# Broadcasting a norm's root with a diagonal and a ones matmul, and copying the rotary key with two DMAs, in a one-core transformer kernel

## The reference, cut to what matters

```python
def rms_norm(x, g):
    xf = x.astype(jnp.float32)
    y = xf * lax.rsqrt(jnp.mean(xf * xf, axis=-1, keepdims=True) + NORM_EPS)
    return (y * g.astype(jnp.float32)).astype(x.dtype)

    o = rms_norm(o, subln_g) * (1.0 - lambda_init)          # diff_attention, for each head
```

```python
    k_pe = apply_rope(proj[..., MLA_Q_RANK + MLA_KV_RANK:], cos, sin)
    ...
        sc = (jnp.einsum('bqhd,bkhd->bhqk', qn, k_nope)
              + jnp.einsum('bqhr,bkr->bhqk', qp, k_pe)).astype(jnp.float32) * scale
```

## Time and profile before

| | us |
|---|---|
| median of 3 runs (1761.54 to 1761.56) | 1761.56 |
| the profiled execution, its own time | 1761.54 |
| its span, first to last instruction | 1759.8 |
| TensorE busy | 1744.0 (99%) |
| VectorE busy | 1104.8 (63%) |
| ScalarE busy | 792.3 (45%) |

### The profile page before, as it was taken

How to read it: one execution, slowest core, us unless ns; L and a number is a source line. 1 busy time by engine, 2 the same in 40 slices (tenths; PEclk the granted TensorE clock), 3 DMA queues, 4 the chain that set the end, 5 groups by cost and what they waited for, 6 DMA issues and landing times.

```text
span 1759.8 us, 22818 instructions
## 1 busy us (share of the span) xinstructions
PE 1744.0 (99%) x8844; PEld 1471.2 (84%) x8844; DVE 1104.8 (63%) x1830; ACT 792.3 (45%) x1418; POOL 129.7 (7%) x129
## 2 busy tenths in 40 slices
PE   9999999999999999999999999999999999999998
PEld 7888888888888888888888888898888888888886
DVE  4689644343346766686755755756989777376375
ACT  6563522222235565545433433457766544144244
POOL 2003200000005100002000000022000200000000
PEclk9999999999999999999999999999999999999999
DMA  5212333333333221223333333323011233333341
GB/s 167 73 49 81 96 96 98 97 99 102 96 96 96 72 61 61 66 67 88 103 96 96 96 96 96 96 77 89 26 61 37 72 96 96 96 96 96 97 128 62
DMA packets 128355, 152.78 MB, mean 87 GB/s; under 512 B 9286, under 2 KB 101992, under 8 KB 128248
## 3 DMA queue, kind: packets, MB, share of 16 engines
q1 hardware_dynamic: 128088, 151.26, 28.1%
q10 hardware_dynamic: 160, 0.07, 0.0%
HBM read 148.61 MB, written 2.10 MB: 86 GB/s over the span
## 4 chain that ended last, share of the span: by engine, by line
PE 96%; DVE 1%; ACT 1%; issue 1%; POOL 0%; DMA 0%; ACTq 0%; POOLq 0%; DVEq 0%
PE bk L1801 23%; PE bk L1803 23%; PE bk L1802 23%; PE bk L1830 6%; PE bk L1832 6%; PE bk L1831 6%; PE bk L1806 4%; PE bk L1901 2%; PE bk L1868 1%; PE bk L1889 1%; PE bk L1891 1%; PE bk L1890 1%; ACT WH L2161 0%; PE bk L1934 0%; PE bk L1935 0%
## 5 line engine op out<-in xcount | busy, mean ns | idle before, releaser
L1801 PE MATMUL bk<-R,WH 128*128 128x512 f32 x1764 | 691.1, 392 | 1.2 <-DVE R L1972 0.9
L1803 PE MATMUL bk<-R,WL 128*128 128x512 f32 x1764 | 686.8, 389 | 0.0
L1802 PE MATMUL bk<-R,WH 128*128 128x512 f32 x1764 | 686.6, 389 | 0.0
L1966 DVE TENSOR_TENSOR WL<-RAW,WH 128x1024 fp32r<-128x1024 f32 (+4 forms) x278 | 343.7, 1237 | 483.9 <-ACT WH L2161 483.0
L2161 ACT ACTIVATE WH<-RAW 128x1024 fp32r<-128x1024 f32 (+4 forms) x278 | 288.0, 1036 | 595.6 <-PE bk L1803 540.0
L1801 PEld LDWEIGHTS bk<-R,WH 128*128 128x128 f32 x1764 | 331.2, 188 | 69.7 <-issue 2.5
L1803 PEld LDWEIGHTS bk<-R,WL 128*128 128x128 f32 x1764 | 331.1, 188 | 69.6
L1802 PEld LDWEIGHTS bk<-R,WH 128*128 128x128 f32 x1764 | 331.3, 188 | 67.0
L1830 PE MATMUL bk<-WH,R 128*128 128x512 f32 (+4 forms) x528 | 186.3, 353 | 0.2 <-ACT TOK L2218 0.2
L1832 PE MATMUL bk<-WL,R 128*128 128x512 f32 (+4 forms) x528 | 178.3, 338 | 0.0
L1831 PE MATMUL bk<-WH,R 128*128 128x512 f32 (+4 forms) x528 | 178.1, 337 | 0.0
(11 more groups left out here) (162 smaller groups left out, 1538.5 us busy)
## 6 DMA issues: line engine op xcount, KB each, us to landing
RAW<-in_ffn_w_up_dram SPq DMA_DIRECT2D x176, 256.0 KB, 3.1
RAW<-in_ffn_w_down_dram SPq DMA_DIRECT2D x44, 512.0 KB, 3.7
RAW<-in_w_gate_dram SPq DMA_DIRECT2D x44, 256.0 KB, 2.9
RAW<-in_w_up_dram SPq DMA_DIRECT2D x44, 256.0 KB, 3.1
RAW<-in_w_down_dram SPq DMA_DIRECT2D x22, 512.0 KB, 3.7
RAW<-in_da_w_qkv_dram SPq DMA_DIRECT2D x32, 256.0 KB, 2.9
RAW<-in_w_out_dram SPq DMA_DIRECT2D x8, 512.0 KB, 3.7
RAW<-in_da_w_qkv_dram SPq DMA_DIRECT2D x8, 512.0 KB, 3.7
```

The costliest lines, as they stand in the source:

```text
L1801: e.matmul(dst, lh, rh, start=start, stop=False)
L1802: e.matmul(dst, lh, rl, start=False, stop=False)
L1803: return e.matmul(dst, ll, rh, start=False, stop=stop)
L1966: e.tensor_tensor(low, RAW[:, r, 0:m], high.bitcast(F32), ALU.subtract).then_inc(on["wlo_dve"], 1)
```

## The change

Two steps are changed. First, `over` no longer transposes. A new VectorE step `diag` multiplies the identity (`IDN`) by each of the four columns of the root, which gives four diagonal 128 by 128 blocks in a slot of `FS`, and `over` multiplies a matrix of ones by each block in plain fp32 on TensorE. Second, `kpe` writes the rotary key's halves only into the first pair of key tiles (36 by 512 instead of 36 by 2048), and two DMAs copy them to the other three pairs of the first group and the four of the second. The `kups` lists are made in `mla_group` instead of ahead of it.

```diff
-    "over": {"pe": 1}, "over_copy": {"act": 1},
+    "diag": {"dve": 1}, "over": {"pe": 1}, "over_copy": {"act": 1},
...
-        return {"add": 682.0, "tap1": 743.0, "tap0": 743.0, "settle": 745.0, "root_in": 165.0, "root_ez": 165.0,
+        return {"add": 682.0, "tap1": 743.0, "tap0": 743.0, "settle": 745.0, "diag": 880.0, "root_in": 165.0, "root_ez": 165.0,
...
-        s_kpe = sem("s_kpe")
+        s_kpe = [sem(f"s_kpe{i}") for i in range(2)]
...
+                dg = yield from fslot()
+                st = yield step("diag", dst=FS[:, dg.i, 0:S], r=r.r1, after=counts([dg.free, r.rooted]))
                 bk = yield from bank()
-                st = yield step("over", bank=bk.i, r=r.r1, after=counts([bk.free, r.rooted]))
+                st = yield step("over", bank=bk.i, src=FS[:, dg.i, 0:S], after=counts([bk.free, st.dve]))
+                fsl.put(dg, st.pe)
...
+            dg = yield from fslot()
+            st = yield step("diag", dst=FS[:, dg.i, 0:S], r=r, after=counts([dg.free, rooted]))
             b3 = yield from bank()
-            st = yield step("over", bank=b3.i, r=r, after=counts([b3.free, rooted]))
+            st = yield step("over", bank=b3.i, src=FS[:, dg.i, 0:S], after=counts([b3.free, st.dve]))
+            fsl.put(dg, st.pe)
...
-            four = BK[b.i][64:100, :].unsqueeze(1).to_broadcast([36, 4, S])
-            lo = yield from halves(KT[64:100, 0:8:2, :], KT[64:100, 1:8:2, :], four, [st.pe], None, counts(kfree[0:8]))
-            for i in range(0, 8, 2):
-                lat.k[i] = lo
+            lo = yield from halves(KT[64:100, 0, :], KT[64:100, 1, :], BK[b.i][64:100, :], [st.pe], None, kfree[0] + kfree[1])
+            lat.k[0] = lo
             put_bank(b, lo)
-            while len(Ms[0].kups) < 4:
-                yield None
-            emit("kpe_copy", i0=8, i1=16, after=counts([lo, Ms[0].kups[3], kfree[8:16]]))
-            ready_at[id(s_kpe), 16] = at_time(Ms[0].kups[3]) + 8500.0
-            for i in range(8, 16, 2):
-                lat.k[i] = (s_kpe, 16)
+            for n, (i0, i1) in enumerate(((2, 8), (8, 16))):
+                emit("kpe_copy", n=n, i0=i0, i1=i1, after=counts([lo, kfree[i0:i1]]))
+                ready_at[id(s_kpe[n]), 16] = at_time(lo) + 4500.0 + 2000.0 * n
+                for i in range(i0, i1, 2):
+                    lat.k[i] = (s_kpe[n], 16)
...
-                        mm = turn(BK[st.bank][:, t * P:t * P + P], st.r[:, t:t + 1].to_broadcast([P, P]))
+                        mm = e.matmul(BK[st.bank][:, t * P:t * P + P], ONES, st.src[:, t * P:t * P + P], start=True, stop=True)
...
+                elif k == "diag":
+                    for done in st.after:
+                        w.wait_ge(*done)
+                    for t in range(4):
+                        i = e.tensor_scalar(st.dst[:, t * P:t * P + P], IDN, st.r[:, t:t + 1], None, ALU.mult)
+                    i.then_inc(on["diag_dve"], 1)
```

More of the change, by code:

```diff
@@ L1497, in kpe @@
             lat.ups.append(st.pe)
-            four = BK[b.i][64:100, :].unsqueeze(1).to_broadcast([36, 4, S])
-            lo = yield from halves(KT[64:100, 0:8:2, :], KT[64:100, 1:8:2, :], four, [st.pe], None, counts(kfree[0:8]))
-            for i in range(0, 8, 2):
-                lat.k[i] = lo
+            lo = yield from halves(KT[64:100, 0, :], KT[64:100, 1, :], BK[b.i][64:100, :], [st.pe], None, kfree[0] + kfree[1])
+            lat.k[0] = lo
             put_bank(b, lo)
-            while len(Ms[0].kups) < 4:
-                yield None
-            emit("kpe_copy", i0=8, i1=16, after=counts([lo, Ms[0].kups[3], kfree[8:16]]))
-            ready_at[id(s_kpe), 16] = at_time(Ms[0].kups[3]) + 8500.0
-            for i in range(8, 16, 2):
-                lat.k[i] = (s_kpe, 16)
-        for G in Ms:
-            G.kups = []
+            for n, (i0, i1) in enumerate(((2, 8), (8, 16))):
[3 more added lines that the diff above has]
+                    lat.k[i] = (s_kpe[n], 16)
         def mla_group(G, g, prior, before):
@@ L1515, in mla_group @@
             G.heads, G.turned = 0, True
-            G.tq, G.tk, G.qups, G.rope = [], [], [], None
+            G.tq, G.tk, G.qups, G.kups, G.rope = [], [], [], [], None
             in_line(G.V, G.O, *[[q] for q in G.Q])
@@ L1776, in sync_program @@
                     src = KT[64:100, 0:2, :].bitcast(F32).unsqueeze(1).to_broadcast(list(dst.shape))
-                    e.dma_start(dst, src).then_inc(s_kpe, 16)
+                    e.dma_start(dst, src).then_inc(s_kpe[st.n], 16)
                 elif st.kind == "lam_load":
```

## The result

The changed kernel takes 1778.68 us (median of 4 runs, 1778.31 to 1779.31) against 1761.55 us before, a ratio of 1.0099 (95% interval 1.0086 to 1.0111). It is slower by 17.1 us. The forecast was 1766.2 us, +4.6 us, with a range up to 1769.6: the sign was right, the size was not, and the range missed.

The account below looks back on a forecast made before the run. TensorE, busy 99% of the span at full clock, was taken to bound the kernel, so its added work is paid in full. 1761.5 + 5.4 + 0.2 + 1.4 - 0.8 - 1.5 = 1766.2 us, range 1763.0 to 1769.6.

Parts of the forecast that it names:

- `over` in fp32: On TensorE, 13 times: four fp32 blocks take 0.86 us instead of 0.45, 5.4 us more in all (4.4 to 6.5).
- Rival 4: On TensorE: over's new form runs in a single pass, four taking 0.24 us; 1756.0 us in all; chance 0.04.
- The last head's chain, +1.4: Last DA head: six product matmuls now ahead of over start it 1.37 us later, so TensorE's wait grows 1.4 us.
- In the norms `over_copy` ends 1.8 us later. ... 0 us: Norms: over_copy's readers are FFN evictions, with some 43 us of work possible before a bank must be free; 0 us.
- The two tight heads, 0.2 in all: Fourth and sixth heads: only some 3.2 us of work covers root and diag; 0.1 us each, bounds 0 and 1.0.
- That fits: 0 us: Ten other places: 4.1 us or more of TensorE work between sums and over covers root and diag; no cost.
- The copies ... Cost 0, with 8 us of room: MLA: two key DMAs issued at about 1202 land by 1210, before head 1's score after 1218; upper bound 1 us.
- Its split is used about 10 us after that: MLA: the split of the weight load behind the copies is used about 10 us after that load lands.
- some 4 us later: MLA, SyncE's queue: the weight load behind the key copies lands some 4 us later, at no cost.
- MLA's gain, -0.8 and -1.5: MLA: earlier tok_k removes TensorE's 0.80 us wait; more cover for the softmax gives -1.5 us (bounds 0 and -3.2).

Follow-up runs that it names:

- over_form: The kernel before with over's four transposes made plain fp32 products of the same operands, no diag and no later start: 1767.78 us, 1.0032 of before.
- over_late: The kernel before with the diag step and an over that waits for it, but over still four transposes: 1767.84 us, 1.0032 of before.
- keys_only: The changed kernel with over turned back to transposes and no diag, so only the rotary key is changed: 1766.00 us, 1.0020 of before.
- over_only: The kernel before with only the broadcast changed (diag and the ones product), its keys as before: 1774.14 us, 1.0066 of before.
- keys_apart: The kernel before with the narrow key split, both copies behind the w_ukv load, the second three loads further down SyncE's queue: 1757.11 us, 0.9973 of before.

## Why the prediction was wrong, step by step

- **`over` in fp32: right.** 0.86 us was forecast, the chain has 0.89; eight instructions each, 104 in all. Term: 5.4 us, by the trace 13 x (0.89 - 0.44) = 5.9, by over_form 5.3. Rival 4 (a single pass) is out. The Trainium skill ("TensorE: Matmul & The Clock Gate", Terms) has the transpose mode four times faster; over_form, which exchanges the mode and keeps the operands, shows twice (0.89 against 0.44 us), so here the rule doesn't hold.
- **The last head's chain, +1.4: right in place and size** (0.89 to 2.26 us; over_late shows it alone). What it lacked is the clock: after the longer wait, 1.6 us of half speed in the changed kernel, on which the forecast has no word.
- **"In the norms `over_copy` ends 1.8 us later. ... 0 us": failed.** I asked who reads the copy and whether a bank is free soon. The question was who needs the bank that `over` itself has. All eight serve products there, and the order puts that bank's product right behind `over`: 0.75 us of wait in each of the two late norms, and by the offsets in over_late, where the form costs nothing, 1.0 us each. The changed kernel's order had it to be read: the product that waits for `over_copy` follows `over` with nothing in between.
- **The two tight heads, 0.2 in all:** no wait for `diag` shows on TensorE at either. But in over_late, where the form costs nothing, the stretch from 567 to 789 us is 2.1 us longer than before, and the list has one wait of size in it, 0.5 us before head turns near 587. The rest is many small distances in an order that has changed, and I haven't settled it. "That fits: 0 us" was true of waits for `diag` and not of the time.
- **"The copies ... Cost 0, with 8 us of room": failed, and it is the largest miss.** The step that failed is who waits for the load behind them. "Its split is used about 10 us after that" asks when the weights are needed; the one who waits is ScalarE, which does its work in order and has the last `tok_k` queued behind the split. In keys_only it stood ready for the split from 1208.4 us (7.05 us before 1215.48), so there was no room at all. The size of the delay was off by less. With the copies in 8 us after their issue and the load "some 4 us later", the load was due 12 us after the copies' issue, and it landed 13.9 us after it. By that estimate the landing as forecast would have held up ScalarE for some 5 us already. (If the 4 us were meant from the load's own issue, they were 12.) I had followed SyncE's queue for the copies' own reader and not for the load behind them, though I wrote that it stood there. By keys_only against keys_behind: 8.1 to 8.5 us. The trace of the kernel before had a warning. Its one copy isn't recorded as landing, but a load of 512 KB is issued 2.2 us behind it, and takes 7.6 us (view of the DMA issues, 1220 to 1229 us) where such loads take 3.7:

```profile
RAW<-in_mla_w_o_dram SPq DMA_DIRECT2D x1, 512.0 KB, 7.6
```

- **MLA's gain, -0.8 and -1.5: right in kind, half the size.** With the copies out of the way the key part gives -4.6 us (keys_behind). TensorE's idle time from 1195 to 1300 us falls from 4.33 to 1.58 us there, which is 2.75 of it; where the rest comes from is not shown. The stretch in the kernel before and in keys_behind (us, PE busy, clock, DMA share, GB/s):

```profile
1195.00:1300.00 105.00, 100.67 (x605) 1.00 0.18 51
```

```profile
1195.00:1300.00 105.00, 103.42 (x635) 1.00 0.23 62
```

In the changed kernel itself the softmax waits are short too (43.82 of 45 us busy from 1240 on), but that was bought by the stop ahead of them.

In one sum, from the runs, each against its own runs of the kernel before: form +5.3, late start +5.4, keys with their copies out of the way -4.6, the held-up load +8.1 are 14.2; over_only stands 1.0 above its two parts, and the half speed at the last head, which the changed kernel's trace has and over_only's has not, is 1.6. That makes 16.8, against 17.1 measured. The intervals of the single terms are some 2 us wide, so that it closes this well is in part luck. The forecast had the first, less than a third of the second, half of the third, and nothing of the rest.

A version that beats both kernels came out of it: keys_behind, before's broadcast with the narrow key split and both copies behind the w_ukv load, 1757.50 us, 0.9972 of before. That is 0.3%, and keys_apart repeats it.

## What to carry to other kernels

When a transfer is moved up a queue, price every transfer behind it, and for each of these ask which engine waits for it in order, and what that engine has queued behind. The reader of the data may have ten microseconds of room while a bystander has none. When an instruction is moved later on a full engine, look at the buffer that it holds: the next user of its bank, not the reader of its result, may be the one that stands.

## What the runs showed of the hardware

- A plain fp32 product of 128 columns costs twice a transpose of the same block and operands: 0.89 against 0.44 us for four.
- Two copies inside SBUF (36 partitions, packets of 4 KB, 1.03 MB) ran at 165 GB/s with 76% of the DMA engines' time (keys_only); a stretch that was mostly a load ran at 240 GB/s with 86% (keys_behind). Issued 0.5 us ahead of the copies, the load of 512 KB landed after 5.5 us. Behind them it landed 13.9 us after the copies' issue on the same queue and 13.5 us after it on another.
- After a wait of 2.26 us TensorE was granted half speed for eight products (0.43 us apart for 0.23) in the profiled executions of two kernels and full speed in two others with the same wait. After a wait of 1.18 us two kernels had such a stretch and two with the same wait had none. After the 6.4 us wait the granted clock was 0.78 of full for 12 us. With the 2.26 us wait filled with products it stayed at full, in the one execution that was profiled.
